# Row sums on VectorE in place of modulation products in layers two to four

## The reference

```python
cond = jax.nn.silu(c)
for i in range(DEPTH):                       # DEPTH = 4
    mod = (cond @ w_mod[i] + b_mod[i])[:, None, :]      # w_mod[i]: 1024 x 3072
    shift, scale, gate = jnp.split(mod, 3, axis=-1)
    h = rms_norm(x, norm_pre_g[i]) * (1.0 + scale) + shift
    o = mixer_i(h, ...)                      # GLA, SGU, FOX, GLA
    x = x + gate * rms_norm(o, norm_post_g[i])
```

## Time and profile before

| stretch | what | TensorE | VectorE | ScalarE | GB/s | clock |
|---|---|---|---|---|---|---|
| 44 to 186 | layer 0, input products | 141.5 | 41.3 | 49.8 | | 1.00 |
| 186 to 229 | layer 0, levels | 37.3 | 35.0 | 5.7 | 381 | 0.92 |
| 229 to 263 | layer 0, chunks | 32.2 | 18.2 | 20.2 | 261 | 1.00 |
| 263 to 315 | layer 0, end | 51.2 | 29.1 | 24.0 | 109 | 1.00 |
| 315 to 446 | SGU, products and mixing | 128.2 | 54.7 | 49.4 | 84 | 1.00 |
| 446 to 506 | SGU, mixing and end | 57.8 | 34.1 | 27.6 | 83 | 1.00 |
| 506 to 655 | FOX, q, k, v | 144.2 | 68.6 | 60.6 | 99 | 1.00 |
| 655 to 776 | FOX, attention | 110.1 | 67.3 | 84.4 | 175 | 0.94 |
| 776 to 872 | FOX, z and end | 93.7 | 41.6 | 40.5 | | 1.00 |
| 1019 to 1070 | layer 3, levels | 45.6 | 37.2 | 10.0 | 369 | 0.90 |
| 1070 to 1094 | layer 3, chunks | 21.9 | 15.4 | 15.0 | 138 | 1.00 |

### The profile page before, as it was taken

How to read it: one execution, slowest core, us unless ns; L and a number is a source line. 1 busy time by engine, 2 the same in 40 slices (tenths; PEclk the granted TensorE clock), 3 DMA queues, 4 the chain that set the end, 5 groups by cost and what they waited for, 6 DMA issues and landing times.

```text
span 3174.8 us, 54076 instructions
## 1 busy us (share of the span) xinstructions
PE 2981.2 (94%) x22916; PEld 2420.0 (76%) x22916; DVE 1669.9 (53%) x2947; ACT 1192.7 (38%) x2156; POOL 307.2 (10%) x449
## 2 busy tenths in 40 slices
PE   7999999999999999978888999999999998999998
PEld 4767887756877688768866788888887876788887
DVE  3245445435442656767656653555566636654444
ACT  4314435446441455433344452111114435642121
POOL 1010020000001000043330010101110100000000
PEclk9999999999999999988889999999999999999999
DMA  6284222280224622000010023333341350033221
GB/s 228 80 304 144 80 88 81 83 298 19 95 79 157 234 102 70 22 24 24 23 68 27 1 73 80 126 126 111 116 153 67 92 96 25 8 100 106 98 101 66
DMA packets 172586, 307.59 MB, mean 97 GB/s; under 512 B 22694, under 2 KB 44007, under 8 KB 172089
## 3 DMA queue, kind: packets, MB, share of 16 engines
q1 hardware_dynamic: 134448, 253.35, 23.7%
q0 software_dynamic: 12048, 40.24, 4.1%
q10 hardware_dynamic: 25849, 10.56, 1.2%
HBM read 295.95 MB, written 6.81 MB: 95 GB/s over the span
## 4 chain that ended last, share of the span: by engine, by line
PE 75%; DVE 14%; ACT 6%; DMA 2%; issue 2%; POOL 1%; ACTq 0%; DVEq 0%; SPq 0%; POOLq 0%
PE psum L419 19%; PE psum L421 19%; PE psum L420 19%; PE psum L962 3%; PE psum L577 2%; PE psum L981 2%; DVE small L1126 2%; PE psum L2509 2%; DVE weights_r L363 2%; DVE arena L873 1%; PE psum L2499 1%; PE psum L996 1%; DVE x_lat L876 1%; ACT feat L686 1%; ACT weights_r L354 1%
## 5 line engine op out<-in xcount | busy, mean ns | idle before, releaser
L363 DVE TENSOR_TENSOR weights_r<-weights,weights_r 128x2048 fp32r<-128x2048 f32 (+1 forms) x161 | 360.0, 2259 | 387.6 <-ACT weights_r L354 387.6
L419 PE MATMUL psum<-feat_r,weights_r 128*128 128x512 f32 (+1 forms) x1536 | 539.1, 351 | 2.2 <-DVE weights_r L363 1.2
L420 PE MATMUL psum<-feat_r,weights_r 128*128 128x512 f32 (+1 forms) x1536 | 536.5, 349 | 0.0
L354 ACT ACTIVATE weights_r<-weights 128x2048 fp32r<-128x2048 f32 (+1 forms) x161 | 302.1, 1896 | 623.0 <-DMA weights<-in_w_ffn_gate 220.1
L421 PE MATMUL psum<-feat_r,weights_r 128*128 128x512 f32 (+1 forms) x1536 | 535.8, 349 | 0.0
L419 PE MATMUL psum<-weights_r,feat_r 128*128 128x512 f32 (+2 forms) x1344 | 522.3, 389 | 12.1 <-DVE feat_r L718 8.8
L421 PE MATMUL psum<-weights_r,feat_r 128*128 128x512 f32 (+2 forms) x1344 | 517.4, 385 | 0.0
L420 PE MATMUL psum<-weights_r,feat_r 128*128 128x512 f32 (+2 forms) x1344 | 516.9, 385 | 0.0
L419 PEld LDWEIGHTS psum<-feat_r,weights_r 128*128 128x128 f32 x1536 | 293.3, 191 | 45.8 <-issue 5.5
L420 PEld LDWEIGHTS psum<-feat_r,weights_r 128*128 128x128 f32 x1536 | 293.3, 191 | 36.4
L421 PEld LDWEIGHTS psum<-feat_r,weights_r 128*128 128x128 f32 x1536 | 292.7, 191 | 37.1
(11 more groups left out here) (510 smaller groups left out, 4199.2 us busy)
## 6 DMA issues: line engine op xcount, KB each, us to landing
weights<-in_w_mod SPq DMA_DIRECT2D x36, 2048.0 KB, 14.3
weights<-in_gla_w_in SPq DMA_DIRECT2D x24, 1024.0 KB, 7.3
arena<-in_w_mod_turned POOLq DMA_DIRECT2D x96, 256.0 KB, 3.0
weights<-in_w_ffn_gate SPq DMA_DIRECT2D x22, 1024.0 KB, 7.4
weights<-in_w_ffn_up SPq DMA_DIRECT2D x22, 1024.0 KB, 5.2
weights<-in_w_ffn_down SPq DMA_DIRECT2D x20, 1024.0 KB, 6.7
weights<-in_fox_w_in SPq DMA_DIRECT2D x16, 1024.0 KB, 7.1
weights<-in_sgu_w_in SPq DMA_DIRECT2D x12, 1024.0 KB, 6.3
```

The costliest lines, as they stand in the source:

```text
L354: act.e.activation(WEI_r[:, s * SLOT + HALF:s * SLOT + HALF + n], WEI_t[:, s * SLOT:s * SLOT + n], ACT.Copy).then_inc(*A.put(("weights", c ...
L363: dve.e.tensor_tensor(WEI_r[:, s * SLOT:s * SLOT + n], WEI_t[:, s * SLOT:s * SLOT + n], WEI_r[:, s * SLOT + HALF:s * SLOT + HALF + n].bitc ...
L419: pe.e.matmul(ps, lh, rh, start=first, stop=False)
L420: pe.e.matmul(ps, lh, rl, start=False, stop=False)
```

## The change

The modulations of layers 1, 2 and 3 (mod 1, 2, 3; nine of the 18 sides) are no longer made by TensorE. `SIDES` holds mods 0 and 4 only: two sides at the start, four in layer 0 (points 0, 2, 4, 6), none in FOX, three in layer 3 (points 0, 2, 4). FOX's scores rotate over four banks.

In their place stand 72 sums (`SUMMED`), one for each 128 of the 9216 columns. The host hands over `w_mod[1:]` turned, so that a row holds the 1024 weights of one value. SP loads 128 such rows, 512 KB as 128 partitions x 4 x 256 with runs of 1 KB, into one of two buffers in parts of the feature tile that the first block doesn't use; the condition lies as a row, the same on all partitions, in a third such place (`COND_ROW`, loaded twice, since layer ends overwrite it). VectorE multiplies row and condition and sums them into one column of `MODC` (`dve_summed`); `dve_summed_bias` adds the biases.

The loads stand in SP's queue behind chosen weight chunks (`summed_behind`); that of sum n waits for sum n - 2, which used the same buffer. The sums stand at fixed places of VectorE's program: 16 in layer 0's input products, 6 at its end, 18 in SGU, 20 in FOX's q, k and v, 8 in its z, 4 at its end.

```diff
...
 ARENA = 13312
-SIDES = [(mod, n0) for mod in range(5) for n0 in range(0, (3 if mod < 4 else 6) * D, 2 * NMAX)]
-SIDES_BEGIN, SIDES_GLA, SIDES_SGU, SIDES_FOX = 2, {0: 6, 3: 5}, 0, 5
+SIDES = [(mod, n0) for mod in (0, 4) for n0 in range(0, (3 if mod < 4 else 6) * D, 2 * NMAX)]
+SIDES_BEGIN, SIDES_GLA, SIDES_SGU, SIDES_FOX = 2, {0: 4, 3: 3}, 0, 0
+SUMMED = [(mod, m) for mod in (1, 2, 3) for m in range(3 * KT)]
+SUMMED_GLA = 2 * KT
 COND_W = 16 + KT * 32
...
                 raw = WEI_t[:, s * SLOT:s * SLOT + q * n].rearrange("p (k n) -> p k n", k=q)
                 sp.e.dma_start(raw, src[:, q0:q0 + q, :]).then_inc(*w_in[s].put(("weights", c, j)))
+            for n in range(summed_behind.get((name, index, n0), 0)):
+                sp_summed(sp)
     def act_split(act, c, between=None):
...
         sp.e.dma_start(CONST[:, :], io["k_const"][:, :]).then_inc(*const_in.put("const"))
+    COND_ROW = FL_plain[:, 0:4, 512:768]
+    SUMMED_W = [grid(FEAT_t[:, 0:FEATS], KT)[:, 4 * h:4 * h + 4, 512:768] for h in range(2)]
+    summed_behind = {
+        ("gla_w_in", 0, 1536): 2, ("gla_w_in", 0, 0): 2, ("gla_w_in", 0, 512): 4, ("gla_w_in", 0, 2048): 2,
+        ("gla_w_in", 0, 2560): 4, ("w_mod", 0, 2048): 2, ("gla_w_out", 0, 512): 8,
+        ("sgu_w_in", 0, 1536): 3, ("sgu_w_in", 0, 0): 3, ("sgu_w_in", 0, 512): 1, ("sgu_w_in", 0, 2048): 3,
+        ("sgu_w_in", 0, 2560): 4, ("sgu_w_out", 0, 0): 4,
+        ("fox_w_in", 0, 512): 4, ("fox_w_in", 0, 1024): 4, ("fox_w_in", 0, 1536): 4, ("fox_w_in", 0, 2048): 4,
+        ("fox_w_in", 0, 2560): 2, ("fox_w_in", 0, 3072): 2, ("fox_w_in", 0, 3584): 4, ("fox_w_out", 0, 0): 4,
+        ("fox_w_out", 0, 512): 2}
+    def sp_cond_row(sp, name):
+        sp.wait_ge(*cond_out.of("first cond"))
+        sp.e.dma_start(COND_ROW, cond_dram[2].rearrange("m p -> (m p)").partition_broadcast(P)).then_inc(
+            *first_cond_in.put(name))
+    def sp_summed(sp):
+        n = summed["sp"]
+        summed["sp"] = n + 1
+        mod, m = SUMMED[n]
+        if n == 0:
+            sp_cond_row(sp, "gla")
+        if n == SUMMED_GLA:
+            sp.wait_ge(*B.of((("end", 0), "turned")))
+            sp_cond_row(sp, "after")
+        if n >= 2:
+            sp.wait_ge(*V.of(("summed", n - 2)))
+        sp.e.dma_start(SUMMED_W[n % 2], io["w_mod_turned"][mod - 1, m * P:(m + 1) * P, :].rearrange(
+            "p (k c) -> p k c", k=4)).then_inc(*first_mod_in[n % 2].put(("summed", n)))
+    def dve_summed(dve, count=1):
+        for n in range(summed["dve"], summed["dve"] + count):
+            mod, m = SUMMED[n]
+            w = SUMMED_W[n % 2]
+            dve.wait_ge(*first_cond_in.of("gla" if n < SUMMED_GLA else "after"))
+            dve.wait_ge(*first_mod_in[n % 2].of(("summed", n)))
+            dve.e.scalar_tensor_tensor(w, w, 1.0, COND_ROW, ALU.mult, ALU.mult,
+                                       accum_out=MODC[:, mod * 24 + m:mod * 24 + m + 1]).then_inc(*V.put(("summed", n)))
+        summed["dve"] += count
+    def dve_summed_bias(dve, mod, m, n):
+        cols = MODC[:, mod * 24 + m:mod * 24 + m + n]
+        dve.chain()
+        dve.e.tensor_tensor(cols, cols, pcol("b_mod", mod * 24 + m, n), ALU.add).then_inc(*V.put())
     def act_begin(act):
         for q in (1, 0, 2, 3):
...
         act.e.activation(cond2[:, :, 0], pcol("c_2", 0, 8), ACT.Silu).then_inc(*A.put())
         act.e.activation(cond2[:, :, 1], pcol("c_ctx_2", 0, 8), ACT.Silu).then_inc(*A.put("cond"))
+        act.chain()
+        act.e.dma_start(cond_dram[2].rearrange("m p -> p m"), cond1[:, :, 0],
+                        allow_slow_non_contiguous=True).then_inc(*cond_out.put("first cond"))
     def pe_begin(pe):
...
         dve_norm_params(dve, pre, *params)
         dve_take(dve)
+        if tag in (("end", 0), ("end", 2)):
+            dve_summed(dve, 4)
         for t in norm_order(pre)[:len(norm_order(pre)) - len(tiles)]:
             dve_norm_scale(dve, pre, t)
...
                 dve.wait_ge(*B.of(at))
                 dve.e.tensor_copy(Y[:, t, 0:NMAX], K.at[at]).then_inc(*V.put(K.frees(V, at), (tag, "y", 0, t)))
+                if tag == ("end", 0) and pair[0] == tiles[0]:
+                    dve_summed(dve)
                 if beside[t] is not None and pair[0] != tiles[0]:
                     dve_low(dve, pre, beside[t])
...
     def dve_gla(dve, i, j):
         T = ("gla", i)
+        sums = 1 if i == 0 else 0
         for n0 in (0, 512):
             dve_take(dve)
...
                 dve.wait_ge(*B.of(at))
                 dve.e.tensor_copy(g_v[:, t, n0:n0 + NMAX], K.at[at]).then_inc(*V.put(K.frees(V, at)))
+                if n0:
+                    dve_summed(dve, sums)
             if n0 == 0:
                 dve_narrow(dve, i)
...
         V.mark((T, "x"))
         dve_take(dve)
+        dve_summed(dve, 2 * sums)
         dve.wait_ge(*A.of((T, "ln")))
         dve.chain()
         dve.e.scalar_tensor_tensor(g_x, g_x, 0.0, g_tmp, ALU.min, ALU.subtract).then_inc(*V.put((T, "log")))
+        dve_summed(dve, 2 * sums)
         for n0 in (0, 512):
             if n0:
...
                     dve.wait_ge(*B.of(at))
                     dve.e.tensor_copy(g_k[:, m - 4, :], K.at[at]).then_inc(*V.put(K.frees(V, at)))
+                    if m < 6:
+                        dve_summed(dve, sums)
         V.mark((T, "qk"))
         for n0 in (0, 512):
             dve_take(dve)
+            dve_summed(dve, 4 * sums)
+        if i == 0:
+            dve_summed_bias(dve, 1, 0, 2 * KT)
         V.mark((T, "in"))
         dve.wait_ge(*B.of((T, "in")))
...
                 dve.wait_ge(*A.of((T, "v", n0, t)))
                 dve.e.bn_stats(s_st[:, t, 6 * h:6 * h + 6], s_v[:, t, n0:n0 + NMAX]).then_inc(*V.put())
+                if t:
+                    dve_summed(dve)
         for t in LAT:
             dve.chain()
...
             dve.chain()
             dve.e.tensor_tensor(s_v[:, t, :], s_v[:, t, :], s_lnb, ALU.add).then_inc(*V.put())
+            dve_summed(dve)
             if t == 0:
                 dve_take(dve)
...
         for n in range(2):
             dve_take(dve)
+            dve_summed(dve, 4)
+        dve_summed_bias(dve, 1, 2 * KT, KT)
+        dve_summed_bias(dve, 2, 0, 2 * KT)
         dve_side(dve, False)
         for t in LAT[:2]:
...
                         dve.chain()
                         dve.e.tensor_copy(f_v[:, t, n0 - 2048:n0 - 2048 + NMAX], K.at[at]).then_inc(*V.put(K.frees(V, at)))
+                        dve_summed(dve)
                     continue
                 r = calls % 2
...
                                [K.frees(V, at), (T, "qn", n0, t)])
                 calls += 1
+                dve_summed(dve)
         V.mark((T, "in"))
         dve.wait_ge(*A.of((T, "in")))
...
                 dve.chain()
                 dve.e.tensor_tensor(o, o, grid(f_zs[t % 2], 4), ALU.mult).then_inc(*V.put((T, "gated", n0, t)))
+                dve_summed(dve)
+            if n0 == 0:
+                dve_summed_bias(dve, 2, 2 * KT, KT)
+                dve_summed_bias(dve, 3, 0, 2 * KT)
...
         T = ("end", i)
         y, name, Y, off = first_y(i)
+        if i == 3:
+            dve_summed_bias(dve, 3, 2 * KT, KT)
         dve_to_feat(dve, T, LAT, before={(0, t - 1): lambda t=t: dve_sgu_mix(dve, t) for t in (2, 3)} if i == 1 else None)
         dve_gate(dve, T, 0, "norm_post_g", i * KT, 2, i)
...
     nc = _bacc.Bacc("TRN2", target_bir_lowering=False, num_devices=1)
     arrays, io = {}, {}
-    turned = {"w_mod_2_turned": _np.asarray(inputs["w_mod_2"])[1].T}
+    turned = {"w_mod_2_turned": _np.asarray(inputs["w_mod_2"])[1].T,
+              "w_mod_turned": _np.asarray(inputs["w_mod"])[1:].transpose(0, 2, 1)}
     for name, a in list(inputs.items()) + list(turned.items()) + list(constants().items()):
         a = _np.ascontiguousarray(a)
```

More of the change, by code:

```diff
@@ L191, in program @@
     keys_in = signal("window_values_in", 16)
+    first_cond_in, first_mod_in = signal("first_cond_rows", 16), [signal(f"first_mod_rows_{h}", 16) for h in range(2)]
     rpb_in, rpb_out, x_out = signal("rpb_in", 16), signal("rpb_out", 16), signal("x_out", 16)
@@ L197, in program @@
     cond_out, cond_in, mod_in = signal("cond_out", 16), signal("cond_rows_in", 16), [signal(f"mod_weights_{h}", 16) for h in range(2)]
-    every = [B, A, V, G, *w_in, cond_out, cond_in, *mod_in, const_in, x_in, ctx_in, *par_in, layer_in, bias_in, keys_in, down_in, rpb_in, rpb_out, x_out,
+    every = [B, A, V, G, *w_in, cond_out, cond_in, *mod_in, first_cond_in, *first_mod_in, const_in, x_in, ctx_in, *par_in, layer_in, bias_in, keys_in, down_in, rpb_in, rpb_out, x_out,
              *spill_out, sums_out, *decay_in, narrow_in, turns_in, *gate_out, *gate_in]
@@ L231, in program @@
     down_dram = nc.dram_tensor("down_spill", [P, NTOK, 416], F32, kind="Internal")
-    cond_dram = nc.dram_tensor("cond_rows", [2, KT, P], F32, kind="Internal")
+    cond_dram = nc.dram_tensor("cond_rows", [3, KT, P], F32, kind="Internal")
```

(6 more changed lines are left out.)

## The result

The changed kernel takes 3217.59 us, the median of four runs (3215.52 to 3218.65), against 3185.56 for the kernel before, the median of four. The ratio is 1.0103, with a 95% interval from 1.0077 to 1.0129: 32 us slower, where 9 us, inside what can't be told from no change, was forecast, in a range that ended at 3216. So neither the size nor the range held. The forecast had the sign, less than a third of the size, and missed the end of its range by 1.6 us; the mechanism of the largest single loss (FOX's products) was the one described.

The account below looks back on a forecast made before the run. TensorE, busy 94%, was taken as the main bound, with each place having its own last wait (VectorE in GLA's levels). Terms -23 +18 +9 +6 +5 -4 -2 gave +9 on 3186.3, so 3195 us, range 3160 to 3216.

Parts of the forecast that it names:

- layer 0, products and scan: First GLA layer: two sides fewer save time, less about 6 us for the output weights' split moving earlier; -4 us.
- end of layer 0: First layer's end: sums before the copies make the normed rows late, TensorE idles 4.0 us, then half clock; +6 us.
- SGU: SGU: second z chunk's load waits for four sums, output chunk's load moves alike, mixing starts 8.6 us later; +9 us.
- FOX q, k, v: FOX's query and key products: sum loads hold weight loads in SP's queue, TensorE waits for VectorE's scale; +18 us.
- attention: FOX's attention: five side products, their folds, a 3.02 us wait and half clock go; -23 us, bounds -28 and -17.
- z and its end: FOX's z: one more gating and sum lengthen TensorE's wait to 4.1 us, plus 2.5 at half clock; +5 us.
- layer 3: Fourth layer (GLA): two sides fewer, one a chunk's and one a level's, less 4 us for the moved split; -2 us.
- the price of a sum: On VectorE: 1.31 us per sum, 94 us for 72; its load lands in 3.9 us, back-to-back turns about 3.9 + 1.3.
- The rival of half pace: VectorE's sum takes 2.46 us rather than 1.31, adding 23 us on the path: 3218 us; chance .03.
- Loads in time: SP's queue: sums end before their chunk, no weight load is late, only savings stay: 3160 us; chance .20.
- Slow sum loads: Sum loads of 1 KB runs land in about 6 us rather than 3.9, adding 14 us: 3209 us; chance .27.
- The copies at 273.81 move to about 276.8.: End of the first layer: four sums before the copies delay them to 276.8, the first tile's normed rows by 7.7 us.

Follow-up runs that it names:

- the experiment with the loads later: Changed kernel, sums unmoved, but their loads one place later in SP's order from SGU on (two or three fewer before a weight chunk): 3184.46 us, ratio 0.9986.

## Why the prediction was wrong

By its own terms, forecast and measured (after minus before in the table):

| term | forecast | measured |
|---|---|---|
| start | none | +7.5 |
| layer 0, products and scan | -4 | -1.1 (scan -4.2, products +3.2) |
| end of layer 0 | +6 | +12.8 |
| SGU | +9 | +13.2 |
| FOX q, k, v | +18 | +15.9 |
| attention | -23 | -22.3 |
| z and its end | +5 | +8.9 |
| layer 3 | -2 | -0.9 (scan -1.2, products +0.3) |
| sum of the layers | +9 | +34.1 |

Right: the attention's saving, from units without a side; the price of a sum; the held queue in FOX, with its delay (10.1 and 8.9) and TensorE's wait (8.4 and 7.93), and the place of the wait in SGU; in the scans, the wait of about 6 behind the split that moved (6.18 and 6.13), and with it the -4, though its size is partly luck (-1.4 to -4.4 over the kernels with four sides). The rival of half pace falls: 1.22 us is the plain pace, 1.23 for a product of that size. Loads in time falls for the kernel after, whose loads leave 8.8 to 11.6 late. Slow sum loads falls by its median, 4.3 and not over 5, but holds at the end of layer 0. The rule of the Trainium skill's Vector Engine (DVE) Microarchitecture Reference, section "Points that are easy to get wrong", that two sources in SBUF that are not bf16 halve this operation's throughput, is not what the trace shows: both sources are float32 in SBUF here. Six sums did take twice as long, beside work of GpSimd, as the last section tells.

Wrong, in the order of size:
- The start. The prediction went through the loads at the start and not through the write that makes the row: 4 KB in pieces of 4 bytes. That step of the change has no term in the sum, and nothing was said why. A row of the trace before could have shown the kind: ten other column writes of 4 KB land after 10.7 us. 7.5 us.
- "The copies at 273.81 move to about 276.8." The section on the price says that sums back to back wait for landings, about 3.9 + 1.3 a turn; at the end of layer 0 it was not applied (nor does the 7.7 that follows come out of the rows named: 3.0 and two sums of 1.31 make 5.6). The six sums took 21 us there, as their loads left one behind the other and three of them took 8.2 to 14.9 to land. Here 6.8 us.
- SGU "+9". The one load that was followed is right. But the output weights' load was taken to move alike; it is held by its own four sum loads as well and leaves 11.6 late. The mixing begins at 479.98, 14.1 later against its own start and not 8.6. 4.2 us more in all; the experiment with the loads later gives back all 13 but 1.4.
- z "+5": up to the first output product the stage loses 4.6, as forecast; the four sums at its end and their loads had no term and cost 4.4 in the output products. 3.9 us more in all. With no sum behind the first chunk the stage is back at 95.4.
- The 3.2 us at half clock in layer 0's input products had no term either, but are not the change's as far as is known: the kernel before shows them too, in one of its two traces.

All of these errors point the same way. The range was made of the rivals' times and not of the terms' bounds, whose upper ends add up to +42, or 3228; it ended at 3216, and the term that was forgotten had no bound at all.

## What to carry to other kernels

A transfer that is freed by late work must not stand in an in-order queue ahead of one that is due earlier: count, for each load in the queue, which event frees it and when, and put it behind the loads that leave before that. Take work off an engine first where that engine is what the stage waits for: five of nine side products gave 23.5 of 29 us. Where a list gets shorter, look at what stands behind its last item: in the scans a split moved up with it, and TensorE waited 6 us behind it. And price every transfer that a change issues by its pieces, not its bytes, above all beside a start that waits for weights.

## What the runs showed of the hardware

A sum takes 1.22 us, but six of the 72 took 2.27 to 2.31, all of them while GpSimd multiplied two tiles in SBUF. Two more, only in part beside such a product, took 1.42 and 1.66. GpSimd's and VectorE's timelines after, in SGU:

```profile
443.33 7.18 POOL L1547 TENSOR_TENSOR arena<-arena 128x512 f32<-128x512 f32 x4 [96.52 <-ACT arena L1600]
```
```profile
443.57 2.31 DVE L566 SCALAR_TENSOR_TENSOR feat<-feat 128x1024 f32<-128x1024 f32 x1
445.82 2.30 DVE L566 SCALAR_TENSOR_TENSOR feat<-feat 128x1024 f32<-128x1024 f32 x1
450.30 1.29 DVE L566 SCALAR_TENSOR_TENSOR feat<-feat 128x1024 f32<-128x1024 f32 x1 [2.18 <-DMA feat<-in_w_mod_turned]
```

The third, past GpSimd's end at 450.51 but for 0.2, is at full pace again. The Trainium skill's page "SBUF — State Buffer", section "Terms", says that VectorE and GpSimd share a pair of ports, that one holds it for a whole instruction and the other stands still. The durations agree with that: the sums took 2.31 and 2.30 rather than 1.22, and the two GpSimd products that lie wholly beside them 2.26 and 2.27 rather than the 1.28 of the fourth.

And a write of 1024 pieces of 4 bytes set the start back by 7.5 to 8.5 us, though it moves 4 KB: 70 GB/s in the stretch from 25 to 30 us where 387 were moved without it.
